# A state-space stage rebuilt on half the time steps, its small products cut into 32-wide strips of TensorE

## The reference, cut to what matters

```python
u, z = split(h @ w_in)                       # both 256 x 2048
ug = u as 128 groups of 16 features          # SSM_GROUPS = 128, SSM_STATE = 64
bu_re, bu_im = ug x bb_re, ug x bb_im        # per group 16 -> 64 complex states
x[t] = a * x[t-1] + bu[t]                    # complex, per group and state, 256 steps
y = Re(x) c_re - Im(x) c_im + d_skip * u     # per group 64 -> 16
y = gelu(y); y = y * sigmoid(y @ w_glu + b_glu)
out = (y * silu(z)) @ w_out;  x = x + gate * out
```

## Time and profile before

| | |
|---|---|
| median of 3 runs | 3552.73 us (3550.99 to 3554.13) |
| profiled execution, span | 3551.0 us; no other time is given for it |
| PE busy | 3347.8 us (94%) |
| DVE busy | 2369.0 us (67%) |
| ACT busy | 1555.3 us (44%) |
| POOL busy | 294.9 us (8%), nearly all of it in the recurrence |
| mean granted TensorE clock | 0.971 |

### The profile page before, as it was taken

The page is one execution under the profiler, slowest core; times in us unless marked ns, Lnnn a source line. Parts: engine busy times, 40 slices in busy tenths (PEclk is TensorE's granted clock), DMA queues, the critical chain, the costliest instruction groups (busy, mean ns, idle before and its releaser), DMA issues. The chain is left out here.

```text
span 3551.0 us, 55886 instructions
## 1 busy us (share of the span) xinstructions
PE 3347.8 (94%) x20020; PEld 2915.5 (82%) x20020; DVE 2369.0 (67%) x2871; ACT 1555.3 (44%) x1935; POOL 294.9 (8%) x293
## 2 busy tenths in 40 slices
PE   7999999999999989999999988778789899999998
PEld 7989898878788879998999778455478798988877
DVE  6757887656656654456645673999975635667765
ACT  6433433554434454433433344454544533455543
POOL 0000000000000000000000001777720000000000
PEclk9999999999999999999999989989899999999999
DMA  6856776458778745558755765122245456744435
GB/s 221 300 191 236 270 274 219 163 184 278 262 242 272 255 162 182 183 183 308 249 183 182 281 228 171 58 77 70 64 145 178 154 198 230 275 149 147 144 130 178
DMA packets 189039, 699.24 MB, mean 197 GB/s; under 512 B 20928, under 2 KB 21184, under 8 KB 187072
## 3 DMA queue, kind: packets, MB, share of 16 engines
q1 hardware_dynamic: 183744, 669.07, 55.2%
q10 hardware_dynamic: 5120, 27.70, 2.2%
HBM read 692.49 MB, written 4.19 MB: 196 GB/s over the span
## 5 line engine op out<-in xcount | busy, mean ns | idle before, releaser
L1744 DVE TENSOR_TENSOR ring_parts<-ring,hi_parts 128x1024 fp32r<-128x1024 f32 x1002 | 1212.1, 1247 | 421.3 <-ACT hi_parts L1041 414.8
L1041 ACT ACTIVATE hi_parts<-ring 128x1024 fp32r<-128x1024 f32 x1002 | 1024.8, 1056 | 673.5 <-DMA ring<-in_stream 669.4
L619 PE MATMUL psum<-arena_low_parts,hi_parts 128*128 128x256 f32 x6048 | 1119.9, 286 | 1.8 <-DVE ring_parts L1744 1.7
L619 PEld LDWEIGHTS psum<-arena_low_parts,hi_parts 128*128 128x128 f32 x6048 | 955.3, 193 | 6.3 <-DVE ring_parts L1744 2.2
L619 PE MATMUL psum<-arena_low_parts,ring_parts 128*128 128x256 f32 x3088 | 876.4, 284 | 0.0
L636 PE MATMUL psum<-hi_parts,arena_high_parts 128*128 128x512 f32 x2304 | 760.2, 395 | 8.2 <-DVE ring_parts L1744 8.1
L636 PE MATMUL psum<-hi_parts,arena_low_parts 128*128 128x512 f32 x2112 | 694.2, 395 | 12.9 <-DVE ring_parts L1744 5.3
L619 PEld LDWEIGHTS psum<-arena_low_parts,ring_parts 128*128 128x128 f32 x3088 | 595.2, 193 | 0.0
L636 PEld LDWEIGHTS psum<-hi_parts,arena_high_parts 128*128 128x128 f32 x2304 | 434.8, 189 | 102.4 <-DVE ring_parts L1744 9.5
L636 PEld LDWEIGHTS psum<-hi_parts,arena_low_parts 128*128 128x128 f32 x2112 | 400.1, 189 | 96.3 <-DVE ring_parts L1744 9.2
L636 PE MATMUL psum<-ring_parts,arena_low_parts 128*128 128x512 f32 x1216 | 476.1, 392 | 0.0
(11 more groups left out here) (309 smaller groups left out, 2944.1 us busy)
## 6 DMA issues: line engine op xcount, KB each, us to landing
ring<-in_stream SPq DMA_DIRECT2D x1272, 512.0 KB, 4.1
arena_high<-in_ssm_bc ACTq DMA_DIRECT2D x17, 640.0 KB, 3.9
arena_high<-in_mem ACTq DMA_DIRECT2D x2, 1024.0 KB, 6.0
arena_high<-in_x ACTq DMA_DIRECT2D x1, 2048.0 KB, 12.0
arena_low<-in_x ACTq DMA_DIRECT2D x1, 2048.0 KB, 7.8
x_kept<-arena_low ACTq DMA_DIRECT2D x1, 2048.0 KB, 6.4
arena_low<-x_kept ACTq DMA_DIRECT2D x1, 2048.0 KB, 7.7
out<-arena_low SPq DMA_DIRECT2D x4, 512.0 KB, 3.7
```

Of the source, the lines that this page charges most:

```text
L619: mm = pe.matmul(bank[:, half:half + S], r32(w[:, slot, cols]), r32(x[part][:, k, :]), start=(k == 0 and n == 0), stop=(k == KT - 1 and n ...
L1041: act.activation(r32(hi[:, g % RING, cols]), ring[:, g % RING, cols], ACT.Copy).then_inc(hi_made, 1)
L1744: dve.tensor_tensor(r32(slot), slot, as32(hi[:, g % RING, cols]), ALU.subtract).then_inc(cut_done, 1)
```

## The change

The recurrence is run on every second time step: with A = a and b = bb, x[2c] = A² x[2c-2] + (A b) u[2c-1] + b u[2c] (written with the powers that the code makes). The states exist at even times only; outputs at odd times are made from the state before by C·A and a direct term. In detail:
- One phase `ss` takes the place of `su` and `sz`: unit su 0, then su 1, sz 0, su 2, sz 1, ... sz 15. Each chunk has two units. The loops are unrolled over 16 chunks.
- TensorE: `prepare` (two transposes, four matmuls of 64 rows x 32 columns of the array, 256 moving columns), `inputs` (16 matmuls of 32 rows, 128 moving columns, four row strips in turn), `direct_terms` (8 matmuls, 32 array columns, 32 moving columns), `outputs` (32 matmuls of 32 array columns, 128 or 127 moving columns, four column strips in turn, and one of 128x128).
- DVE: `products`, `rotated` (was POOL's), `scans` (8 of 128 steps), `back` work on 128 steps; `fractions`, `turned`, `direct_block` are new.
- ACT: `prepared`, `turns`, `tables`, `inputs_turned` on 128 steps; the gelu is applied to 8, 6 and 2 chunks at once. POOL makes only the C matrices.
- B comes as four 32-row pieces beside C, five DMAs a chunk. `xr` stays on chip; both transfers of x_kept go.
- In `av`, a new part of `s5_params` (12 instructions on DVE) and `s5_rows` (two transposes and an ACT copy). `BEFORE_S5` is preceded by `turns(0)`, `prepared(0)`, `load(2)` on ACT, `fractions(0)`, `turned(0)` on DVE and `prepare(0)` on TensorE.

```diff
-    ("fo1", FF_PARTS[1], 8), ("su", 16, 8), ("sz", 16, 32), ("glu", 16, 8), ("so", 16, 8),
+    ("fo1", FF_PARTS[1], 8), ("ss", 32, 68), ("glu", 16, 8), ("so", 16, 8),
...
+            def prepare(cc):
+                bank = free_bank(prep_bank(cc))
+                pe.wait_ge(ssm_landed[cc % 2], 16 * SSM_DMAS * (cc // 2 + 1))
+                for part in range(2):
+                    pe.transpose(bank[:, 256 + part * P:256 + (part + 1) * P], ssm_b(cc)[:, part, :], ident[:, :])
+                for q in range(PAIRS):
+                    n = PAIRS * cc + q
+                    mm = pe.matmul(bank[32 * q:32 * q + 32, 0:256], ident[0:64, n:n + 1].broadcast_to([64, 32]), aT,
+                                   start=True, stop=True)
+            def inputs(cc):
+                pe.wait_ge(ssm_u_ready, cc + 1)
+                pe.wait_ge(ssm_ab_ready, cc + 1)
...
+                for part in range(2):
+                    for s, b in enumerate((turned_b[cc % 2], ssm_b(cc))):
+                        for q in range(PAIRS):
+                            rows = slice(32 * q, 32 * q + 32)
+                            mm = pe.matmul(psum[:, 4 + q, part * HS:(part + 1) * HS], b[rows, part, :],
+                                           ssm_u[cc % 2][rows, s, :], start=(s == 0), stop=(s == 1))
+            def direct_terms(cc):
...
+                for m in range(2):
+                    for q in range(PAIRS):
+                        rows = slice(32 * q, 32 * q + 32)
+                        mm = pe.matmul(bank[rows, 256:288], b_turned[cc % 2][:, m, rows], ssm_w[cc % 2][:, m, q, :],
+                                       start=(m == 0), stop=(m == 1))
+            def outputs(cc):
+                bank = free_bank(y_bank(cc))
+                pe.wait_ge(ssm_back, cc + 1)
+                terms = ((0, 0, 0), (0, 1, 1), (1, 0, 1), (1, 1, 0))
+                for m, (k, x, part) in enumerate(terms):
+                    for q in range(PAIRS):
+                        pe.matmul(bank[32 * q:32 * q + 32, HS:2 * HS], ssm_w[cc % 2][:, k, q, :], back_q[x][:, q, part, :],
+                                  start=(m == 0), stop=(m == 3))
+                pe.matmul(bank[:, 0:HS], direct, ssm_u[cc % 2][:, 0, :], start=True, stop=False)
...
+            for cc in range(SSM_CHUNKS):
+                if cc + 1 < SSM_CHUNKS:
+                    t_unit("su", cc + 1, h3T, own_bank=su_bank(cc + 1))
+                if cc + 2 < SSM_CHUNKS:
+                    prepare(cc + 2)
+                t_unit("sz", cc, h3T, own_bank=sz_bank(cc))
+                if cc + 1 < SSM_CHUNKS:
+                    inputs(cc + 1)
+                    direct_terms(cc + 1)
+                outputs(cc)
...
+            load(0)
+            load(1)
+            steps(FFN_OUT[1])
...
+            turns(0)
+            prepared(0)
+            load(2)
             steps(BEFORE_S5)
+            tables(0)
+            cut(POS[("unit", "su", 0)] + LEAD)
+            inputs_turned(0)
+            prepared(1)
+            load(3)
+            turns(1)
+            for cc in range(SSM_CHUNKS):
+                if cc + 1 < SSM_CHUNKS:
+                    cut(POS[("unit", "su", cc + 1)] + LEAD)
+                    if cc >= 2 and cc + 2 < SSM_CHUNKS:
+                        act.wait_ge(ssm_in_done, cc + 1)
+                        act.wait_ge(ssm_w_ready, cc + 1)
+                        load(cc + 2)
+                    tables(cc + 1)
+                    inputs_turned(cc + 1)
+                if cc + 2 < SSM_CHUNKS:
+                    prepared(cc + 2)
+                cut(POS[("unit", "sz", cc)] + LEAD)
+                if cc + 2 < SSM_CHUNKS:
+                    turns(cc + 2)
+                act.wait_ge(*multiplied("sz", cc))
+                act.activation(zT[1][:, cc, :], stream_bank(sz_bank(cc))[:, 0:S],
+                               ACT.Silu).then_inc(evacuated[sz_bank(cc) % 4], 2 if cc == SSM_CHUNKS - 1 else 1)
+                if cc in GELU_AT and cc < SSM_CHUNKS - 1:
+                    gelus(*GELU_AT[cc])
...
+            for cc in range(SSM_CHUNKS):
+                later = cc + 1 < SSM_CHUNKS
+                products(cc)
+                if cc:
+                    did(skip(cc - 1))
+                direct_block(cc)
+                if cc == 0:
+                    turned(1)
+                if later:
+                    fractions(cc + 1)
+                dve.wait_ge(ssm_prod, cc + 1)
+                rotated(cc, 0)
+                rotated(cc, 1)
+                if later:
+                    cut(POS[("unit", "su", cc + 1)] + LEAD, halves_=(0,))
+                did.wait()
+                scans(cc, 0)
+                if later:
+                    cut(POS[("unit", "su", cc + 1)] + LEAD, halves_=(1,))
+                scans(cc, 1)
+                did.wait()
+                did(back(cc, 0))
+                back(cc, 1).then_inc(ssm_back, 1)
+                cut(POS[("unit", "sz", cc)] + LEAD)
+                if cc + 2 < SSM_CHUNKS:
+                    turned(cc + 2)
```

More of the change, by code:

```diff
@@ L90 @@
     _list = [("unit", _name, _u) for _u in range(_units)]
+    if _name == "ss":
+        _list = [("unit", "su", 0)]
+        for _u in range(1, _units // 2):
+            _list += [("unit", "su", _u), ("unit", "sz", _u - 1)]
+        _list += [("unit", "sz", _units // 2 - 1)]
     _with = [x for x in MOD_RUNS if _name in x[0]]
@@ L243 @@
 FFN_OUT = [spread("fo0"), spread("fo1")]
-BEFORE_S5 = [("norm", "x2", j) for j in range(KT // 2)] + spread("su")
+BEFORE_S5 = [("norm", "x2", j) for j in range(KT // 2)]
 def with_gate(phase, tag):
@@ L926, in outputs @@
[L926 to L943, removed]
[L944 to L949 removed]
+            def prepare(cc):
[7 more added lines that the diff above has]
+                                   start=True, stop=True)
+                mm.then_inc(ssm_prepared, 1)
@@ new lines, in _ @@
+            prepare(0)
+            steps(BEFORE_S5)
+            t_unit("su", 0, h3T, own_bank=su_bank(0))
+            prepare(1)
+            inputs(0)
+            direct_terms(0)
+            for cc in range(SSM_CHUNKS):
[8 more added lines that the diff above has]
+                outputs(cc)
@@ L1261, in _, with load @@
                                            ACT.Silu).then_inc(ff_gate, 1)
-                steps(FFN_OUT[part])
+                if part == 0:
+                    steps(FFN_OUT[0])
+            def load(cc):
+                dst = bc_first[cc] if cc < 2 else bc_later[cc % 2]
+                for q in range(PAIRS):
+                    rows, cols = slice(32 * q, 32 * q + 32), slice(256 * q, 256 * q + 256)
+                    act.dma_start(dst[rows, 0:256], A["ssm_bc"][cc, rows, cols]).then_inc(ssm_landed[cc % 2], 16)
+                act.dma_start(dst[:, 256:512], A["ssm_bc"][cc, :, SSM_B:SSM_COLS]).then_inc(ssm_landed[cc % 2], 16)
@@ new lines, in inputs_turned, with gelus @@
+            def inputs_turned(cc):
+                last = cc == SSM_CHUNKS - 1
+                b = su_bank(cc)
+                act.wait_ge(*multiplied("su", cc))
+                if cc >= 2:
+                    act.wait_ge(*emptied(y_bank(cc - 2)))
+                act.activation(ssm_u[cc % 2], by_parity(stream_bank(b)[:, 0:S]), ACT.Copy).then_inc(ssm_u_ready, 1)
+                act.wait_ge(ssm_u_ready, cc + 1)
+                act.nop().then_inc(evacuated[b % 4], 2 if last else 1)
+            def gelus(first, end):
+                act.wait_ge(*emptied(y_bank(end - 1)))
+                part = uT[:, first:end, :].rearrange("p c t -> p (c t)")
+                act.activation(part, part, ACT.Gelu_apprx_tanh).then_inc(ssm_gelu, 1)
@@ new lines, in scans, with back @@
+            def scans(cc, half):
+                for q in (2 * half, 2 * half + 1):
+                    col = s5[:, S_MAG2, PAIRS * cc + q:PAIRS * cc + q + 1]
+                    for part in range(2):
+                        z = rot[0][:, q, part, :]
+                        did(dve.tensor_tensor_scan(z, col.broadcast_to([P, HS]), z, 0.0, ALU.mult, ALU.add))
+            def back(cc, half):
+                qs = slice(2 * half, 2 * half + 2)
+                did(dve.tensor_tensor(back_q[0][:, qs], rot[0][:, qs], cos_t[cc % 2][:, qs], ALU.mult))
+                ins = dve.tensor_tensor(back_q[1][:, qs], rot[0][:, qs],
+                                        sin_t[cc % 2][:, qs].unsqueeze(2).broadcast_to([P, 2, 2, HS]), ALU.mult)
+                return ins
```

401 lines of the change are left out of this document (193 added, 208 removed).

## The result

| | before | changed |
|---|---|---|
| median | 3553.03 us (3550.99 to 3554.13) | 3342.23 us (3322.8 to 3346.68), 4 runs |
| ratio, with 95% interval | | 0.9394 [0.9368, 0.942] |
| profiled execution | span 3551.0 us | 3339.5 us, span 3337.7 us |
| first matmul of the stage to glu | 504.3 us | 2102.91 to 2393.84: 290.9 us |

The kernel became 211 us faster. The case that happened is rival B (the strips run beside each other, DVE bounds), and B's own price, 3360 us, was 18 us too high.

What follows compares the result with a forecast made beforehand. DVE bounded the old recurrence at 24.6 us a chunk; PE would bound the new stage at 20.7 against DVE's 18.6. With the ends, glu starts at 2444 instead of 2608, span 3551.0 - 163 = 3388, so 3390 us, range 3350 to 3490.

Steps and rivals of the forecast that it cites:

- rival B: Recurrence stage: strips run fully beside each other on PE, DVE bounds at 18.6 us a chunk; 3360 us, chance 0.24.
- What bounded before, and which stage gains: Before, DVE set the recurrence's pace at 24.6 us a chunk; the stage, 504.3 us to glu, is what the change rebuilds.
- PE's chunk of 20.7 us: TensorE's work per chunk in the new stage: two units 11.6 us, the rest strip matmuls at about half their serial time.
- a value between the bounds: The forecast itself: PE's strips overlap about twofold, between 27.1 and 16.3 us a chunk; 3390 us, own range 3370 to 3412.
- DVE's chunk of 18.6 us: DVE's work per chunk: instructions 16.7 us, waits for its own results 0.8, POOL's cost 1.1; between 16.7 and 21.1.
- POOL's price of 1.1 us: DVE's loss per chunk to POOL in the stage: 3.6 us of POOL work at 0.30 us lost for each.
- ACT at nothing: ACT's 12.7 us a chunk in the stage costs nothing, hidden by DVE and PE; without cover showing only from 19 us.
- The head: Ahead of the stage: DVE does fractions(0) and turned(0), 1.8 us, after rms, so su starts 2.0 us late, at 2105.7.
- x_kept, B's five DMAs, the clock: Dropped x_kept transfers give nothing; B's DMAs land in about 3.9 us, ahead of prepare; clock near 1.00.
- Rivals A and D: In the stage, A: strips in turn, PE 27.1 us, 3492 us, chance 0.17; D: clock falls to 1.2 GHz, 3721 us, 0.04.
- C: Rival: PE and DVE don't hide each other in the stage, 2 to 4 us more a chunk, 3422 to 3454 us, chance 0.14.
- The signs I named: Profile signs: PE over 95% busy if right; DVE 99% for B; 7 us outputs for A; cuts still 2 us if wrong.

Runs made afterwards that it cites:

- e4: Changed kernel with POOL computing nothing from the third chunk on, so the outputs use stale matrices: 3314.76 us, ratio 0.9334.
- e8: The changed kernel with no edit, timed and profiled again: 3330.47 us, ratio 0.9376; stage 272.2 us, chunk 16.34 us.
- e2: Changed kernel with outputs() going through all four products of one column strip before the next strip: 3358.72 us, ratio 0.9452.
- e9: Changed kernel with both inputs and outputs strip by strip, the strip as the outermost loop: 3386.39 us, ratio 0.9531.
- the second: Profile of the unedited changed kernel taken again later: stage 272.2 us, span 3320.0 us; its median was 3330.47 us.

## Why the prediction was right and wrong

- **What bounded before, and which stage gains**: right. From the first matmul of the stage to glu it is 290.9 us instead of 504.3. The glu row moved by 214.2 us, the span by 213.3, so the gain lies in the stage.
- **The step that failed: PE's chunk of 20.7 us.** I assumed "that the second pass of a matmul needs the strip that its first pass holds; then the next strip's first pass can only run beside a second pass". All four strips run beside each other instead, first passes included: the four first passes of `prepare` start within 0.02 us, 0.24 us ahead of any second pass. From start to next start in e4, outputs took 2.0 us and not 3.5, inputs 1.1 and not 2.8, prepare 0.6 and not 0.9, direct_terms 0.15 and not 0.8. My own sum for this case was 16.3 us, the 0.6 for changes of shape included; where PE paces the stage without an edit to its order (e8, e4) the chunk is 16.34, and with the strips in turn it is 16.34 + 1.65 + 2.75 = 20.74 against 20.73 measured. No row of before showed two strips, and the one measurement at hand, the Trainium skill's 3.07 times, spoke for the four; I gave that case 0.24 and a value between the bounds 0.41. The choice between 27.1 and 16.3 was not a matter of degree: the forecast stood on a mechanism that I had made up to lie between them.
- **DVE's chunk of 18.6 us**, the bound in the first profile, was 17.9 us there. Two terms were too high. A scan of 128 steps takes 0.34 us where I took 0.45, 0.9 us a chunk. My 0.84 for 256 steps came from the earlier trace rows, where POOL works beside it; so POOL was in the price of the scan and was then charged again. Of the 128 scans before, the 16 that ran with no POOL instruction beside them took 0.66 us, with 0.58 to the next start:

```profile
2295.65 0.66 DVE L1943 TENSOR_TENSOR_SCAN arena_high<-s,arena_high 128x256 f32<-128x256 f32 x1
```

  The waits for its own results, 0.8 us, are already inside the distances from start to start. What DVE needs by itself is 15.74 us (e4) against my 16.7 + 0.8. B put glu at 2414, 20.2 us too late: its products begin at 2111.84 instead of 2116, and from there to the end of the last `back` (2388.67) it is 276.8 us against 292.6.
- **POOL's price of 1.1 us** was too low for the first profile: 17.9 - 15.74 = 2.2 us a chunk, for 65.40 / 14 = 4.7 us of POOL (I had 3.6), 0.47 per us and not 0.30. Part of this is the scan again: with 0.58 instead of 0.84 a chunk of before would need 17.2 us, and the 7.4 left for POOL's 18.0 are an estimated 0.41 per us. The rest was hidden by the average: the loss depends on what DVE does meanwhile.
- **ACT at nothing**: right. It was busy 139.73 us of 250, 10.0 us a chunk, against my 12.7, and waited 96.8 us for DVE's fractions.
- **The head**: su began 13.7 us after the start of rms instead of 10.65, so 3.0 us and not 2.0. rms took 4.50 us instead of 3.26: three of its eight instructions, those beside POOL's first two combinations at 2089.85 and 2090.60, took 0.79 to 0.95 us instead of 0.48. All ahead of rms was 3.7 us earlier in this profile, but that is no gain: rms starts anywhere from 2086.3 to 2094.8 in the profiles of the edits, and the span less the stage is the same as before.
- **x_kept, B's five DMAs, the clock**: right. No engine waits for a DMA in the stage, and the granted clock is 0.97 where PE has gaps and 1.00 where it has none (e2, e9). Rivals A and D did not happen. C's time did not either, but one of its mishaps did, "a DVE held longer by POOL": in the first profile the chunk is 1.6 us above what PE needs and 2.2 above what DVE needs.
- **The signs I named** were good ones: "B would show DVE at 99% and PE waiting for back" is what the profile has. "Cuts on DVE still at 2 us" came true as well, as 4.06 for a pair in every fourth chunk of the first profile. Moving POOL was worth 12 to 23 us of time, and in the stage 21 us against the first profile and 3 against the second.

## What to carry to other kernels

If a cost depends on a question that no row answers (do strips overlap?), work out the answer at either end, and give most of the chance to the end for which a measurement exists. A made-up middle is a third mechanism and needs its own evidence. Where GpSimd must work beside a busy VectorE, place it by a wait under VectorE's operations out of PSUM: here that gave 12 to 23 us for one wait, and it made the times steadier. A row from beside GpSimd holds GpSimd's price already; look for one without it before adding the price.

The best version is the changed kernel with POOL behind `turned_b`: 3318.77 us in five rounds, 0.9345 [0.9332, 0.9357] of before.

## What the runs showed of the hardware that was not expected

- fp32 matmuls in two passes overlap across four strips almost fully: 32 passes of 128 columns take 1.07 us with the strips interleaved, 1.54 by pairs, 2.44 strip by strip, and would take 3.5 if every step were the 0.11 of one strip.
- A scan's price goes by its length: 0.39 us for 128 steps, 0.66 for 256, 1.21 for 512, with no POOL instruction beside it. Beside POOL the same 256 steps took 0.82 to 1.21 us.
- A POOL operation and a DVE operation with two inputs in SBUF both lose when they overlap, as if they took turns. In the chunk shown the two engines work side by side from 2197.34 to 2202.88, 5.5 us. DVE's cuts and `turned`'s first pair lost 2.8 us in it (4.06 + 1.84 against 2.35 + 0.75), POOL's four instructions 2.5 us (3.53 + 1.60 + 0.92 against 2.06 + 0.74 + 0.74).
- DVE out of PSUM does not notice POOL (0.68 us in both). The instruction of rms, with one large input in SBUF, does: 0.79 to 0.95 us instead of 0.48.
